# Scores of the meta queries: two products per piece with four stationary columns, low rows added once

## What is computed

```
q = concat(q_nope, rope(q_rope)); k likewise          # (T=1040, 8 heads, 96)
s = einsum('bqhd,bkhd->bhqk', q, k) / sqrt(96)
y = einsum('bhqk,bkhd->bqhd', softmax(s), v)
```

## Time and profile before

| | us |
|---|---|
| three executions timed | 1299.99, 1302.21, 7115.12; median 1302.21 |
| the profiled execution's own time | 1303.02 |
| its span in the profile | 1301.2 |
| TensorE busy in it | 1271.2 (98%) |
| VectorE, ScalarE, GpSimd busy | 996.9 (77%), 769.3 (59%), 146.6 (11%) |

### The profile page before, as it was taken

How to read it: one execution, slowest core, us unless ns; L and a number is a source line. 1 busy time by engine, 2 the same in 40 slices (tenths; PEclk the granted TensorE clock), 3 DMA queues, 4 the chain that set the end, 5 groups by cost and what they waited for, 6 DMA issues and landing times.

```text
span 1301.2 us, 18506 instructions
## 1 busy us (share of the span) xinstructions
PE 1271.2 (98%) x6158; PEld 1018.6 (78%) x6158; DVE 996.9 (77%) x1505; ACT 769.3 (59%) x1156; POOL 146.6 (11%) x175
## 2 busy tenths in 40 slices
PE   7999999899999999999999999999999999999998
PEld 7999997666666666687678888888888888888886
DVE  6677569678887876577779887887878887887855
ACT  7487648567765866534445565656474565656460
POOL 3000037400000001322200000000010000000010
PEclk9999999999999999999999999999999999999999
DMA  6111200000000014200144846576574847576667
GB/s 220 34 53 41 74 1 1 1 1 10 9 9 10 9 58 155 69 30 1 49 148 94 187 100 166 118 169 134 151 169 93 189 97 169 113 170 133 157 143 245
DMA packets 40938, 123.01 MB, mean 95 GB/s; under 512 B 7378, under 2 KB 8082, under 8 KB 34484
## 3 DMA queue, kind: packets, MB, share of 16 engines
q0 software_dynamic: 7200, 52.43, 21.4%
q1 hardware_dynamic: 33684, 69.86, 15.7%
HBM read 62.34 MB, written 59.80 MB: 94 GB/s over the span
## 4 chain that ended last, share of the span: by engine, by line
PE 85%; DVE 6%; ACT 5%; issue 2%; DMA 1%; POOL 0%; SPq 0%; DVEq 0%; ACTq 0%
PE banks L2911 30%; PE banks L2983 14%; PE banks L100 7%; PE banks L102 7%; PE banks L101 7%; PE banks L1935 2%; PE banks L2040 2%; PE banks L2041 2%; PE banks L2042 2%; PE banks L2060 2%; PE banks L2063 2%; PE banks L2061 2%; ACT e_f L1558 1%; PE banks L1895 1%; ACT e_h L1565 1%
## 5 line engine op out<-in xcount | busy, mean ns | idle before, releaser
L2911 PE MATMUL banks<-x_hi,slot_h 128*128 128x512 f32 x616 | 242.8, 394 | 2.5 <-DVE slot_l L2599 1.3
L2911 PE MATMUL banks<-x_lo,slot_h 128*128 128x512 f32 x616 | 243.4, 395 | 0.0
L2911 PE MATMUL banks<-x_hi,slot_l 128*128 128x512 f32 x616 | 242.9, 394 | 0.0
L2384 ACT ACTIVATE slot_h<-up_raw 128x512 fp32r<-128x512 f32 x127 | 79.8, 629 | 174.4 <-PE banks L2911 172.3
L2911 PEld LDWEIGHTS banks<-x_hi,slot_h 128*128 128x128 f32 x616 | 115.6, 188 | 30.9 <-DVE slot_l L2599 2.1
L2911 PEld LDWEIGHTS banks<-x_lo,slot_h 128*128 128x128 f32 x616 | 115.7, 188 | 27.1
L2911 PEld LDWEIGHTS banks<-x_hi,slot_l 128*128 128x128 f32 x616 | 115.7, 188 | 26.9
L2462 ACT ACTIVATE staged<-banks 128x1024 f32<-128x1024 f32 x100 | 101.4, 1026 | 41.0 <-PE banks L2983 41.0
L2983 PE MATMUL banks<-dn_h,a_h 128*128 128x512 f32 x280 | 110.4, 394 | 0.0
L2983 PE MATMUL banks<-dn_h,a_l 128*128 128x512 f32 x280 | 109.5, 391 | 0.0
L2983 PE MATMUL banks<-dn_l,a_h 128*128 128x512 f32 x280 | 109.5, 391 | 0.0
(11 more groups left out here) (346 smaller groups left out, 2861.5 us busy)
## 6 DMA issues: line engine op xcount, KB each, us to landing
down_sums<-staged POOLq DMA_DIRECT2D x50, 1024.0 KB, 8.0
up_raw<-in_w_up SPq DMA_DIRECT2D x88, 256.0 KB, 3.3
dn_raw<-in_w_down SPq DMA_DIRECT2D x22, 512.0 KB, 6.6
win_raw<-in_w_in SPq DMA_DIRECT2D x11, 512.0 KB, 3.3
x_tm<-in_x_tm SPq DMA_DIRECT2D x8, 512.0 KB, 6.0
wo_raw<-in_w_out SPq DMA_DIRECT2D x16, 256.0 KB, 4.1
h<-in_x_tm SPq DMA_DIRECT2D x8, 512.0 KB, 5.7
down_sums<-h SPq DMA_DIRECT2D x3, 1024.0 KB, 6.6
```

The costliest lines, as they stand in the source:

```text
L2384: nc.scalar.activation(s_h[slot], x, ACT.Copy).then_inc(sem["up_hi"], 1)
L2911: ins = nc.tensor.matmul(o, s[slot][:, k], xs[w], start=fresh and k == 0 and n == 0, stop=k == 3 and n == 2, skip_group_check=not fresh)
```

## The change

The meta queries' stationary operand becomes four columns: the two high and the two low queries side by side. They stand in the last four columns of q_h (1036 to 1039), so that one product with k_h and one with k_l make four rows: the high queries' scores and the low queries' scores, each with the whole key. Job tm writes only the two meta queries, high ones into columns T-4 and T-3 of q_h, low ones into T-2 and T-1, where it wrote 16 columns of q_h and of q_l. ScalarE copies four rows of each piece into x_one. SyncE's queue moves rows 0 and 1 into x_all as before and, by a second transfer, rows 2 and 3 into a new tile x_low of 16 rows. In head 7 VectorE adds x_low to x_all ahead of the reduction. The counts waited for on x_in double. The product of low by low, which was left out, is now part of the sum.

```diff
-    x_one = place("x_one", M_ATT + 2 * T, (T,))[QK:QK + 2]
+    x_one = place("x_one", M_ATT + 2 * T, (T,))[QK:QK + 4]
+    x_low = place("x_low", M_ATT + 4 * T + 3 * T, (T,))[QK:QK + NX]
...
-                sp.dma_start(x_all[2 * h:2 * h + 2], x_one).then_inc(sem["x_in"], 16)
+                sp.dma_start(x_all[2 * h:2 * h + 2], x_one[0:2]).then_inc(sem["x_in"], 16)
+                sp.dma_start(x_low[2 * h:2 * h + 2], x_one[2:4]).then_inc(sem["x_in"], 16)
...
-                nc.scalar.activation(q_h[b][0:QK, SEQ:T], side[0:QK, 0:META], ACT.Copy, scale=gain["q"])\
+                nc.scalar.activation(q_h[b][0:QK, T - 4:T - 2], side[0:QK, META - 2:META], ACT.Copy, scale=gain["q"])\
...
-                        act.wait_ge(sem["x_in"], 16 * h)
+                        act.wait_ge(sem["x_in"], 32 * h)
...
-                nc.scalar.activation(x_one[:, 512 * c:512 * c + w], side[0:2, 0:w], ACT.Copy)\
+                nc.scalar.activation(x_one[:, 512 * c:512 * c + w], side[0:4, 0:w], ACT.Copy)\
...
-                low(q_l[b][:, SEQ:T], side[0:QK, 0:META], gain["q"], q_h[b][0:QK, SEQ:T])
+                low(q_h[b][0:QK, T - 2:T], side[0:QK, META - 2:META], gain["q"], q_h[b][0:QK, T - 4:T - 2])
...
-                dve.wait_ge(sem["x_in"], 16 * HEADS)
+                dve.wait_ge(sem["x_in"], 32 * HEADS)
                 x_m = x_v[QK:QK + NX, 3, 0:1]
+                link(nc.vector.tensor_tensor(x_all, x_all, x_low, ALU.add))
                 link(nc.vector.tensor_reduce(x_m, x_all, AX.X, ALU.max))
...
-                ks, qs = slice(512 * c, 512 * c + w), slice(T - 2, T)
+                ks = slice(512 * c, 512 * c + w)
...
-                nc.tensor.matmul(side[0:2, 0:w], q_h[b][0:QK, qs], k_h[b][0:QK, ks], start=True, stop=False)
-                nc.tensor.matmul(side[0:2, 0:w], q_l[b][:, qs], k_h[b][0:QK, ks], start=False, stop=False)
-                ins = nc.tensor.matmul(side[0:2, 0:w], q_h[b][0:QK, qs], k_l[b][:, ks], start=False, stop=True)
+                q_parts = q_h[b][0:QK, T - 4:T]
+                nc.tensor.matmul(side[0:4, 0:w], q_parts, k_h[b][0:QK, ks], start=True, stop=False)
+                ins = nc.tensor.matmul(side[0:4, 0:w], q_parts, k_l[b][:, ks], start=False, stop=True)
```

## The result

The changed kernel takes 1304.67 us at the median (8 runs, 1301.08 to 1309.31) against 1300.80 for the kernel before; the ratio is 1.0034, interval 1.0023 to 1.0046. That is no change by the 2% mark, as predicted, and 1304.67 lies in the range. But the forecast was a difference of +0.9 us and the ratio says +4.4 us (0.0034 times 1300.8; 3.0 to 6.0 by the interval). The interval excludes +0.9, so the study asks for the other 3.5. That 1304.67 is only 1.6 from the predicted 1303.1 is in part luck: the prediction started from 1302.21, which is 1.4 above the 1300.80 measured here. Executions that fell far out (two of 7115 us of the kernel before, one of 1554 us in experiment 6) are in no ratio and no mean.

A forecast was written before the change was run, and what follows sets the result against it. TensorE is 98% busy, but where the pieces stand the chain runs through ScalarE and VectorE. Removed products -0.3 plus addition 1.27 make +0.9 us (rounded) on the median 1302.21: 1303.1 us, range 1298.8 to 1306.5.

The forecast's parts named there:

- The pieces: One of three TensorE products goes in each of 24 pieces: 3.9 us spared, 0.3 taken to reach the end.
- Kept: 0; lost: 5 times 0.49: Heads 1, 2, 3, 4 and 6: spared product time all becomes longer waiting for k_l and x0's copy; nothing gained.
- The addition: VectorE's addition ahead of head 7's reduction: 1.27 us, reaching TensorE in full; bounds 0 and 2.4.
- What costs nothing: ScalarE's four-row copies, job tm's shorter instructions and SyncE's second transfer per head (0.62 of queue, hidden): 0.
- Rival 1: TensorE's saving counts in full, addition hidden: 1298.3; milder form, 0.3 kept: 1301.9. Chance 0.22 with the milder form.
- Rival 2: Head 7: GpSimd's yl_l starts before VectorE's addition, which then takes some 2.3: +2.1, 1304.3 us. Chance 0.12.
- Rival 3: Wider idling at 502.28 or 247.94 lets TensorE's clock fall once more, 1.7 us: +2.7, 1304.9. Chance 0.16.
- band of +0.3 to +1.6: Whole kernel: the forecast's own span of difference in us against the kernel before, chance 0.50.

The follow-up runs named there:

- experiment 6: Changed kernel with 8 tiny two-column products added behind head 0's x2, to move later instruction transfers: 1305.76 us, ratio 1.0047.
- experiment 3: Kernel before with a second transfer of the same two rows per head into x_low, no addition, three products: 1299.88 us, ratio 1.0001.
- experiment 12: Changed kernel with an overwritten third product in every piece and without VectorE's addition: 1299.75 us, ratio 0.9996.
- experiment 1: Changed kernel without VectorE's addition, low rows collected but left out of the scores: 1302.78 us, ratio 1.0022.
- experiment 4: Changed kernel with the addition moved to GpSimd, VectorE waiting for it: 1303.80 us, ratio 1.0026.
- experiment 8: Changed kernel with the addition on GpSimd and 20 tiny two-column products behind head 0's x2: 1302.83 us, ratio 1.0023.
- Experiment 7: Kernel before with one product per piece (high by high) and 40 tiny products, no second transfer, no addition: 1304.51 us, ratio 1.0037.
- experiment 9: Changed kernel with a third product back in every piece, its result overwritten by the next: 1301.35 us, ratio 1.0014.
- Experiment 2: Kernel before with four linked additions of a tile of zeros to x_all ahead of the reduction: 1304.37 us, ratio 1.0047.
- experiment 10: Changed kernel with three more overwritten products in every piece of head 5 alone: 1305.41 us, ratio 1.0036.
- experiment 11: Kernel before with two more 512-column products ahead of x1's first product in each of heads 1 to 6: 1302.11 us, ratio 1.0011.
- experiment 5: Changed kernel with 20 tiny two-column products added behind head 0's x2, to move later instruction transfers: 1304.67 us, ratio 1.0040.

## Why the prediction was right, and where its sum was wrong

Four kernels make a square: third product there or not, addition there or not. Mean time (standard error), lost clock behind it, in us.

| | no addition | addition | addition's price |
|---|---|---|---|
| third product there | 1299.90 (0.59), 5.4 | 1301.97 (0.50), 6.2 | 2.1 |
| third product gone | 1302.70 (0.56), 7.9 | 1304.68 (0.92), 9.5 | 2.0 |
| price of its going | 2.8 | 2.7 | |

The upper left is the kernel before in all that counts (1300.00, 5.3). The two prices add up to the change, 4.7, and each is the same in either line, within errors of 0.8 to 1.1. Two more pairs stand beside the left column. Three products and nothing that delays x_row: 1300.00, 1299.90 and 1299.90, lost clock 5.3, 5.2 and 5.4 (before, experiments 3 and 12). Two products and nothing that delays it: 1302.70, 1303.23 and 1302.61, lost clock 7.9, 8.6 and 7.2 (experiments 1, 4 and 8).

- **The pieces: the term that failed.** The prediction had them at -0.3. Its reading of the waits was right step by step: x1 and tk1 wait for the same releasers, longer by what the products were shorter, and the span without the lost clock moves by +0.3 without the addition (1292.61 to 1292.88) and by -0.6 with it (1293.90 to 1293.29), both inside the errors. What failed is "Kept: 0; lost: 5 times 0.49": swallowed work was priced at nothing. Taking it away costs 2.7 to 2.8 us in the time, and 2.5 to 3.3 us of lost clock. At 0.63 us of time for one us lost, the clock makes 1.6 to 2.1 of that price; no run shows where the other 0.7 to 1.2 go, if they are not noise. Experiment 7 goes the same way: with three, two and one product per piece and no addition the lost clock is 5.4, 7.9 and 10.4.
- **The addition: right, and a little short.** 1.27 reaches TensorE in full, by 8.54 and 9.81 from mark to mark; four additions brought 6.07. The means say 2.0 to 2.1. The difference, 0.7 to 0.8, is within the errors; the lost clock rises by 0.8 and 1.5 when the addition comes, and experiment 9's trace has a fall behind the longer wait, which fits, but is no more than a hint.
- **What costs nothing: right** (experiments 3 and 12).
- **Rival 1**, the saving counts in full: out, by experiments 1 and 7. **Rival 2**, GpSimd first: did not happen; the addition came 0.14 ahead of yl_l. Experiment 2 shows it real, 0.98 for the addition that meets yl_l. The Trainium skill, "SBUF — State Buffer", section "SBUF: two separate sides", names an exclusive lock held by whichever began first; the rows of 2.26 and 2.22 agree with that.
- **Rival 3**, the clock: this is what happened, under another condition and at another size. The measured +4.4 lies outside the band of +0.3 to +1.6, and above this rival's +2.7; the range took it in only because it had room for rivals 2 and 3 together. The prediction looked for the fall behind one long wait, 502.28 or 247.94, at one fall of 1.7. The changed kernel's trace has no fall at 506.58, where the wait grew to 1.65; experiment 9's has one there behind 1.67, so such a wait can bring a fall and need not. Over the executions the extra lost clock comes to 4.2 us. The square ties 2.5 to 3.3 of that to the removed products, whose waits grew by 0.23 each. The Trainium skill, "TensorE: Matmul & The Clock Gate", section "Part 1: The HAM clock gate", says that the clock follows activity, which the square agrees with, and that the moment of a change varies between runs, which the profiled execution of before (9.1 lost, by its 0.993, where the mean is 5.3) and the table below agree with.
- **Not in the prediction at all**: head 6's two waits from instruction transfers. They are real and cost little in the time.

Which heads do the extra falls lie in? The profiled executions show head 5 best. Sorted by what the clock lost there (between 418 and 432 us), and by the start of the fall, counted from the start of the 18 two-column products:

| products per piece | no fall | 1.7 us lost, start 2.4 to 2.8 us behind | 3.4 us lost, start 3.2 to 3.6 us behind |
|---|---|---|---|
| three (five in experiment 10) | experiments 2, 3, 9, 10, 12 | before, experiment 11 | none |
| two or one | none | experiments 1, 5 | after, experiments 4, 6, 7, 8 |

All seven kernels with fewer products have a fall there, and two of the seven others. But the size goes with the moment at which the fall starts, and at the earlier moment both kinds lose the same 1.7. The moment differs from execution to execution, and no kernel with three products was profiled with a fall at the later one. So these single profiles can't tell the missing products from the moment; what ties the price to the products is the means over 8 to 12 executions each.

Still open: in which heads the extra falls lie on average, what makes the part of the price that the clock does not, why experiments 5, 10 and 11 are 1.3 to 1.8 us longer, lost clock taken off, than the like kernels without their extra products, and whether GpSimd's addition with the third product kept would come back to 1299.9. That last was not run.

## What to carry to other kernels

Work of TensorE that a wait swallows is not free to remove: it may be part of what holds the clock. Here 3.9 us of such products, most of them beside waits of about half a microsecond, cost 2.7 us when they went. Put a price on taking products out of such a stretch, and test by putting a redundant one back. One profile holds one draw of where the clock falls, so before two profiles are compared, look at the mean granted clock of many executions: the profiled execution of the kernel before lay 3.0 us above its mean, and the whole change costs 4.7. And compare executions of one kernel before lost clock is turned into time: here one us lost was worth 0.63.

## What had not been expected of the hardware

- A kernel with redundant products ran faster: 24 products more, 2.7 us less (1301.97 against 1304.68), with a granted clock of 0.9952 against 0.9928.
- It did not work the other way: 12 products put into remaining waits of the kernel before left the lost clock at 5.5 us and made it 2.1 us slower by the means.
- Instructions come in packets of 16 KB through the same 16 DMA engines, about 1.2 us of one engine each. Beside one of them TensorE's wait for the 4 KB row transfer went from none to 1.0 us, and beside another the time from the issue of w_out's loads to ScalarE's conversion of the piece went from 3.8 us (474.60 to 478.36) to 4.8 (475.03 to 479.82). A change of 48 instructions moved them there, 8 tiny products more took one of the waits away and 20 both.
